# One-hot arrays of the expert routing: VectorE makes a group of eight weighted rows with two wide operations in place of eight narrow ones

## The reference, cut to what matters

```
s1 = einsum('nhd,kd->nhk', q[:, :, 0], k_sub1)        # 8 heads, 128 keys
s2 = einsum('nhd,kd->nhk', q[:, :, 1], k_sub2)
v1, i1 = top_k(s1, 16);  v2, i2 = top_k(s2, 16)
cand = v1[..., :, None] + v2[..., None, :]             # 256 sums a head
sc, pos = top_k(cand, 16)                              # 16 experts a head
idx = (i1 * 128 + i2) at pos;  wts = softmax(sc)
out = sum over the 8 * 16 experts of  wts * gelu(u_exp[idx] . x) * v_exp[idx]
```

## Time and profile before

| | |
|---|---|
| median of 3 runs | 5174.52 us (5168.31 to 5177.56) |
| the profiled execution: its own time | 5176.31 us |
| its span, first to last instruction | 5174.7 us |
| TensorE clock granted, mean over the span | 0.967 |
| tile 0's one-hot arrays | 2779.6 to 2841.5 us |
| tile 1's | 2841.5 to 2903.8 us |
| tile 2's, until VectorE is done with them | 2903.8 to 2961.3 us |
| first transfer of `experts()` | 2990.2 us |

### The profile page before, as it was taken

The page is one execution under the profiler, slowest core; times in us unless marked ns, Lnnn a source line. Parts: engine busy times, 40 slices in busy tenths (PEclk is TensorE's granted clock), DMA queues, the critical chain, the costliest instruction groups (busy, mean ns, idle before and its releaser), DMA issues. The chain is left out here.

```text
span 5174.7 us, 59886 instructions
## 1 busy us (share of the span) xinstructions
PE 4849.2 (94%) x23049; PEld 4014.8 (78%) x23049; DVE 3266.7 (63%) x4442; ACT 1471.1 (28%) x1965; POOL 1457.6 (28%) x1042
## 2 busy tenths in 40 slices
PE   6899999999998898998994589999999999999998
PEld 2577777778886656887783579999999899999997
DVE  2222111216765253233558979999999999999997
ACT  4331111222223121222324623233232323323333
POOL 0000000000000131000004835555555555555541
PEclk7999999999999999999996889999999999999999
DMA  9324434443333474323402699999999999999997
GB/s 385 145 93 152 172 144 162 155 149 112 103 111 110 168 265 151 124 82 125 147 32 52 141 343 399 394 396 398 401 397 398 402 400 395 396 395 396 397 391 268
DMA packets 417923, 1273.54 MB, mean 246 GB/s; under 512 B 129876, under 2 KB 154340, under 8 KB 335226
## 3 DMA queue, kind: packets, MB, share of 16 engines
q1 hardware_dynamic: 311972, 630.22, 33.8%
q0 software_dynamic: 96112, 618.32, 29.9%
q10 hardware_dynamic: 9616, 22.02, 1.3%
HBM read 1175.54 MB, written 96.00 MB: 246 GB/s over the span
## 5 line engine op out<-in xcount | busy, mean ns | idle before, releaser
L230 PE MATMUL ps<-w_hi,act_hi 128*128 128x512 f32 x3040 | 1207.8, 397 | 46.0 <-DVE w_lo L225 16.5
L231 PE MATMUL ps<-w_lo,act_hi 128*128 128x512 f32 x3040 | 1191.1, 392 | 0.0
L232 PE MATMUL ps<-w_hi,act_lo 128*128 128x512 f32 x3040 | 1189.9, 391 | 0.0
L225 DVE TENSOR_TENSOR w_lo<-w_stage,w_hi 128x2048 fp32r<-128x2048 f32 x152 | 347.9, 2289 | 749.9 <-ACT w_hi L221 748.9
L230 PEld LDWEIGHTS ps<-w_hi,act_hi 128*128 128x128 f32 x3040 | 575.2, 189 | 201.6 <-issue 54.9
L2534 PE MATMUL ps<-act_hi,x_hi 128*128 128x384 f32 x2048 | 692.5, 338 | 37.3 <-DVE x_lo_early L2689 29.2
L2506 POOL DMA_INDIRECT u_ring<-u_exp,idx_all x256 | 541.1, 2114 | 544.6 <-DVE u_ring L2706 469.4
L2535 PE MATMUL ps<-act_lo,x_hi 128*128 128x384 f32 x2048 | 690.1, 337 | 0.0
L2506 POOL DMA_INDIRECT v_ring<-v_exp,idx_all x256 | 527.2, 2060 | 508.7 <-DVE acc L2725 457.6
L232 PEld LDWEIGHTS ps<-w_hi,act_lo 128*128 128x128 f32 x3040 | 574.8, 189 | 122.2
L231 PEld LDWEIGHTS ps<-w_lo,act_hi 128*128 128x128 f32 x3040 | 575.6, 189 | 116.8 <-issue 1.5
(11 more groups left out here) (354 smaller groups left out, 6300.7 us busy)
## 6 DMA issues: line engine op xcount, KB each, us to landing
w_stage<-w_in SPq DMA_DIRECT2D x96, 1024.0 KB, 5.4
u_early<-u_turned SPq DMA_DIRECT2D x129, 512.0 KB, 8.8
u_early<-v_exp SPq DMA_DIRECT2D x128, 512.0 KB, 9.6
w_stage<-w_ada SPq DMA_DIRECT2D x48, 1024.0 KB, 8.4
ada_st<-w_ada SPq DMA_DIRECT2D x48, 1024.0 KB, 8.1
x_stage<-u_turned SPq DMA_DIRECT2D x85, 512.0 KB, 9.4
x_stage<-v_exp SPq DMA_DIRECT2D x85, 512.0 KB, 9.6
d_w<-w_buf SPq DMA_DIRECT2D x6, 4096.0 KB, 20.8
```

Of the source, the lines that this page charges most:

```text
L225: dve.tensor_tensor(w_lo[:, q % 2], w_in_st[:, q], w_hi[:, q % 2].bitcast(F32), ALU.subtract).then_inc(w_split, 1)
L230: pe.matmul(out, lhs[0], rhs[0], start=first, stop=False)
L231: pe.matmul(out, lhs[0], rhs[1], start=False, stop=False)
L232: return pe.matmul(out, lhs[1], rhs[0], start=False, stop=last)
```

## The change

VectorE's groups of `one2` (three of each four) are made by two TENSOR_TENSORs of 128 x 1024: a comparison of the broadcast `iota` with the eight tokens' second keys (`second_equal`), written to the ring slot, and a product in place with the broadcast weights (`second_weigh`). The product waits for the comparison by a new semaphore, `s_equal`. The wait for the ring slot stands ahead of the comparison. In `extra`, a group's comparison is ahead of VectorE's `one1` group, if it has one, and the product behind it; by the tables above no Q has both, so the two always follow each other directly. POOL's groups of `one2` stay with `second_hot` and its eight TENSOR_SCALARs.

```
+        def second_equal(dve, Q):
+            if Q >= RING2:
+                dve.wait_ge(w_ready, 2 * (Q - RING2) + 2)
+            t, q = divmod(Q, NQ)
+            dve.tensor_tensor(one2[:, Q % RING2], iota.unsqueeze(1).broadcast_to([P, 8, P]),
+                              id_t[:, t % 2, 1, 8 * q:8 * q + 8].unsqueeze(2).broadcast_to([P, 8, P]),
+                              ALU.is_equal).then_inc(s_equal, 1)
+
+        def second_weigh(dve, Q):
+            t, q = divmod(Q, NQ)
+            dve.wait_ge(s_equal, makers(SECOND_BY, Q)[1])
+            dve.tensor_tensor(one2[:, Q % RING2], one2[:, Q % RING2],
+                              id_t[:, t % 2, 2, 8 * q:8 * q + 8].unsqueeze(2).broadcast_to([P, 8, P]),
+                              ALU.mult).then_inc(s_one2["dve"], 1)
...
                     if q == 0:
                         dve.wait_ge(id_taken, t + 1)
+                    by_dve = makers(SECOND_BY, Q)[0] == "dve"
+                    if by_dve:
+                        second_equal(dve, Q)
                     if makers(FIRST_BY, Q)[0] == "dve":
                         first_hot(dve, "dve", Q)
-                    if makers(SECOND_BY, Q)[0] == "dve":
-                        second_hot(dve, "dve", Q)
+                    if by_dve:
+                        second_weigh(dve, Q)
```

More of the change, by code:

```diff
@@ L2106, in route @@
         s_ex, s_exd, gate, route_done = sem("r_ex"), sem("r_exd"), sem("r_gate"), sem("r_done")
-        id_ready, id_taken, s_dist = (sem("r_" + n) for n in ("idready", "idtaken", "dist"))
+        id_ready, id_taken, s_dist, s_equal = (sem("r_" + n) for n in ("idready", "idtaken", "dist", "equal"))
         s_one1 = {who: sem("r_one1" + who) for who in ("act", "pool", "dve")}
```

## The result

The changed kernel takes 5225.1 us (median of 4 runs, 5216.0 to 5230.3), the kernel before 5176.0 (median of 4): a ratio of 1.0094, 95% interval 1.0078 to 1.0110, so 49 us more. The forecast was 5221 us and +46. The profiled execution has a span of 5228.7 us. About 3 us of its excess come from ahead of `route()`: its one-hot arrays start at 2783.0 and not at 2779.6. From that start to the first transfer of `experts()` it is 260.0 us, against 210.6 before; `experts()` takes 2185.7 us after and 2184.5 before. The change is in the stage, and nothing is given back later.

What follows compares the result with a forecast made beforehand. The prediction took POOL, as much as VectorE, to bound the one-hot tiles of route(), whose growth reaches the total in full. Terms 17.7 + 15.4 + 13.2 = 46.3 us on 5174.5 gave 5221 us, range 5197 to 5248.

Steps and rivals of the forecast that it cites:

- POOL as the second bound: In route()'s one-hot tiles, POOL's work plus its wait at the tile's turn is the whole tile: 58.06 + 3.80 = 61.9 us.
- the turn: POOL's serial wait between tiles, through TensorE, last copies and turned keys: 3.8 and 6.2 us before, 4.5 assumed after.
- What holds POOL: POOL nearly stands still while VectorE reads two arrays, as in lines 2327, 2329 and 2118; beside TENSOR_SCALAR it hardly does.
- The price of a pair: Each VectorE comparison and product costs POOL 0.85 + 0.65 = 1.5 us; with twelve pairs, +17 us a tile.
- the relief: About 1 us a tile that POOL regains because VectorE's narrow TENSOR_SCALARs no longer run beside it.
- Rival B: VectorE and POOL block each other for full lengths; POOL loses 2.35 us a pair, total 5251 us; chance 0.14.
- Rival A: POOL is not held by short pairs, or not on the path; only VectorE's 9 us remain, 5183 us; chance 0.10.
- VectorE's own price: A pair takes VectorE 2.50 us against 2.14 for eight narrow operations: 0.36 a group, 4.3 a tile, 13 in all.
- Two ways to the end: From tile 2's start, the stage ends by VectorE's work at 96.4 us or by the last w_buf write at 99.6.
- the write's way: POOL done 73.6 us into tile 2, then 4.4 for its last group, 20.7 write, 0.9 barrier: 99.6, +13.2.
- VectorE's way: In tile 2 VectorE waits before group 13's one1, finishes groups at 67.5 us, then routes tile 4 in 28.9: 96.4.
- +17.7, +15.4 and +13.2: Microseconds added by tile 0, tile 1, and tile 2 to the end of the stage; sum 46.3 us.

Runs made afterwards that it cites:

- Experiment 4: Changed kernel with POOL leaving out three quarters of its operations from tile 1 on: 5195.8 us; earlier, POOL's one1 groups given to ScalarE: 5210.2 us.
- Experiments 1 and 3: Changed kernel with each wide operation reading one array from PSUM, 5181.2 us; changed kernel with comparison and product as eight narrow operations each, 5219.9 us.
- experiment 6: Kernel before, long two-array VectorE operations reading one array from PSUM: 5174.2 us; same in changed kernel: 5182.3; first run plus one VectorE group given to POOL: 5171.4.
- experiment 1: Changed kernel with the comparison's row of numbers and the product's weights each read from a copy in PSUM: 5181.2 us, ratio 1.0015.
- Experiment 5: Changed kernel with the last w_buf write cut into four: 5234.5 us; with that write cut to a quarter of the keys, same 256-byte pieces: 5218.8 us.
- experiment 2: Changed kernel with the comparison left wide and the product made by eight narrow TENSOR_SCALARs: 5210.8 us, ratio 1.0069.

## Why the prediction was right

- **POOL as the second bound.** The step that decided the sign was to add POOL's busy time and the turn, and to find that they make the whole tile although POOL is not touched by the change. Experiment 4 shows it: 79.2 against 63.2 us.
- **What holds POOL.** Read from lines 2327, 2329 and 2118: VectorE's reading of two SBUF arrays. Experiments 1 and 3 separate it from width, count and busy time, and experiment 6 shows it for the operations on which the reading was made.
- **The price of a pair.** Forecast 1.5 us less the relief; POOL grew by 75.5 - 58.1 = 17.4, 75.3 - 56.2 = 19.1 and 75.0 - 56.6 = 18.4 us (tile 2: 2942.87 to 3017.84), forecast 17. Rival B, full holding of both, would have been 27 a tile. Rival A would have been some 5183 us, a time that came out only where PSUM took the cause away.
- **VectorE's own price.** It was over-estimated, without effect on the sum, in which POOL's time makes tiles 0 and 1. A pair takes 2.48 us in the mean of 36, forecast 2.50. But the 2.14 us of a narrow group were read from two quick ones; over all 36 it is 2.06 to 2.43, 2.22 in the mean. So the price is 0.26 us a group and 9 us in all, where the forecast had 0.36 and 13, and 6 us where POOL does not lengthen the product (experiment 1).
- **The turn.** 4.5 us assumed for both; 5.2 and 3.9.
- **Two ways to the end.** VectorE was done with its groups 68.4 us after tile 2's start (forecast 67.5), and `experts()` started 100.1 after it (99.6). Experiment 5 shows the write to be the last, with 2.7 us. On the write's way two misses offset each other in part: POOL was done after 75.0 us (73.6), and its last group was through 3.5 us later (4.4).
- **Luck on VectorE's way.** The 67.5 us were reached by a wait that did not happen. The forecast had VectorE held ahead of group 13's `one1` until POOL's fifth group, 54.7 us into the tile, was through TensorE. POOL ended that group at 49.5 us (2992.39 - 2942.87), and VectorE came to group 13's `one1` at 58.4 without any wait. It had waited at groups 5 and 9 instead, 3.6 and 4.6 us:

```profile
2960.47 1.23 DVE L2118 TENSOR_TENSOR one<-kc,id_t 128x1024 f32<-128x1024 f32 x1 [3.57 <-PE ps L2200]
...
2976.68 1.32 DVE L2118 TENSOR_TENSOR one<-kc,id_t 128x1024 f32<-128x1024 f32 x1 [4.58 <-PE ps L2200]
...
3001.30 1.22 DVE L2118 TENSOR_TENSOR one<-kc,id_t 128x1024 f32<-128x1024 f32 x1
```

- **The terms.** +17.7, +15.4 and +13.2 came out as 80.6 - 61.9 = 18.7, 79.2 - 62.3 = 16.9 and 100.1 - 86.4 = 13.7 us.

The rule of the Trainium skill (SBUF — State Buffer, section "SBUF: two separate sides") agrees with these runs on POOL's side, and on what it is that holds POOL: two SBUF inputs, not one. That the other engine fully blocks, on VectorE's side, differs from them: with 36 pairs beside POOL at work the products took 1.22 to 1.36 us against an even 1.22, and the slowest comparison 1.37 against 1.20. The most in any run is 0.29 us, one operation over 128 x 2048 in experiment 1 with 2.58 us against 2.29. So VectorE never gave up a full POOL operation of 0.6 to 0.8 us.

## What to carry to other kernels

Fusing narrow operations into a wide one with a second tensor in place of a scalar turned, here, an operation that slows GpSimd a little into one that holds it. Before it, ask what runs on GpSimd at that time, and whether that engine's busy time plus its serial hand-over already fills the loop. Where a two-array operation on VectorE is wanted beside GpSimd, one of the two arrays in PSUM removed the standstill here at no price in time per operation (1.22 us either way); the copies into PSUM cost a short operation a tile.

## What the hardware showed that I had not expected

- A narrow TENSOR_SCALAR of 128 x 128 took VectorE 0.22 us of busy time with one per-partition scalar (experiment 2) and 0.29 with two (the kernel before).
- A TENSOR_TENSOR of 128 x 1024 took 1.22 us with one array from PSUM, as with both in SBUF.
- Between two operations on VectorE that both read two SBUF arrays, POOL got in at each of the 39 gaps of 0.03 us in the changed kernel's one-hot arrays and finished one operation beside the second. Where they followed without a gap, it stayed held in 26 of 27 cases; in the one other, at 2898.36, the second took 1.37 us.
- A write from SBUF to DRAM in pieces of 64 bytes moved 87 GB/s, in pieces of 256 bytes 218 GB/s.
